# The eight gate columns from the unnormalised input, in four column groups of TensorE

## The chip, the cores and the metric

The kernel runs on one core of a Trainium2 chip. The metric is the device time of one execution in microseconds (us). TensorE is called PE here, VectorE DVE, ScalarE ACT, GpSimd POOL and SyncE SP.

## The reference, cut to what matters

One inference step of a hybrid decoder layer over 592 rows: 16 meta tokens, 512 prompt tokens and 8 samples of 8 tokens. All data are fp32.

```
xn = x * rsqrt(mean(x*x) + eps) * g              # g = norm1_g
z  = xn @ w_in + b_in                            # 1024 inner
u, q, k, v, o, ipre, fpre, ga, gb = split(z)     # ipre, fpre: 4 columns each, one per head
uc = causal_conv4(u); ha = RG-LRU(uc)            # gates of 16 diagonal blocks, then a scan
hb = mLSTM(q, k, v, ipre, log_sigmoid(fpre))
merged = sigmoid(ga)*(ha @ w_branch_a) + sigmoid(gb)*(hb @ w_branch_b)
x = x + merged @ w_out;  x = x + ConvFFN(RMSNorm(x));  y = RMSNorm(x)
```

The change is about the eight columns `ipre` and `fpre`, called the gates below. The mLSTM needs them much later than the first 50 us.

## The kernel before, in words

The input lies transposed in SBUF, features on the 128 partitions, 592 rows along the free dimension, as 8 tiles of 128 features. A large product is made from three fast (fp32r) products: the weight is split in a high part (`whi`) and a low part (`wlo`), the input in `xh` and `xl`, and high*high, high*low and low*high are summed in PSUM. One unit tile of 128 output columns is one `gemm`: 8 k-steps of 3 products, each in two column halves, 48 matmuls (line 2063). Its weight comes by DMA into `stage`, ACT copies it into `whi` (`hi`, line 963) once the tile two before is done, POOL subtracts to get `wlo` (`lo`, line 905, counted by `w_lo`). ACT evicts the tile. Two PSUM areas of two banks (`wide[0]`, `wide[1]`) alternate by the tile's number; four more banks (`bank`) serve everything else.

The start of the kernel, up to the second unit tile, is written out by hand, in order, for each engine:

- PE turns the raw input (`turn`, `late_turn`, line 2101). It is done in 16 jobs: job n is feature tile n % 8, columns 0 to 255 for n < 8 (part 0) and 256 to 591 for n >= 8 (part 1).
- For each job ACT keeps the raw data (`raw_copy`, line 1015, into `x_raw`), DVE scales them out of PSUM by norm1_g and by the row `rrow` of inverse roots (`xn_scaled`, line 1432, `tile_evicted`), ACT rounds to `xh` (`xn_high`, line 1027), and POOL (part 0, line 917) or DVE (part 1, line 1468, `xn_lo_b`) makes `xl`. PSUM has four slots for these jobs, so `late_turn(n)` waits for the scaling of job n - 4.
- Between the turns PE does the gates (`gate_step`, 16 steps of three matmuls with 36 stationary columns; ten of them stand ahead of `late_turn(15)`) and the first unit tile (`first_step`, 16 steps of three), both in line 2110. A gate step or first step of job n waits for that job's `xl`.
- `row_transposes` (line 2091) turns 15 tiles of parameter rows into PSUM in two groups; ACT copies them into `cols` (`columns`, line 1033).
- `keep_clock` are transposes whose result nobody reads.

Then the unit tiles 1 to 15 follow in a loop over g. Ahead of g = 3 stands `lru_gates(0)` (line 2209), which uses all four banks of `bank` and waits for `conv(0)`.

On DVE, after the last `xl`, the order is: copies from `cols`, `lru_rates()`, `conv(0)`, `conv(1)`, and then the loop. `lru_rates` sends |lambda| to ACT, waits for ACT's exp (`lam_exp`, line 1090), and goes on with some twenty operations on 8 columns, each waiting for the one before. `conv(f)` is one TENSOR_SCALAR (line 1552) and three SCALAR_TENSOR_TENSOR (line 1432) over 616 columns and waits for the eviction of unit tile f.

On ACT, after the 16 jobs: `hi(2)` (line 963), `columns` of both groups, the two evictions of the gates into `gs` (lines 1085, 1087), the exp of lambda, and then for each g: `lru_period(g)`, `main_hi(g)` (the split of weight g + 3, which waits for the end of unit tile g), and the eviction of unit tile g.

Of the kernel before, what the change touches and what calls it, by code (L numbers as in the profile page):

```python
# [31 lines left out]
P = 128  # L32
KT = D // P
# [54 lines left out]
T_GATE = T_COLS2 + 2  # L88
T_U = T_GATE + 1
# [167 lines left out]
def hybrid_layer(nc, a, o):  # L257
    w_in, b_in = a["w_in"][0], a["b_in"][0]
    ctx = ExitStack()
    with ctx:  # L260
# [128 lines left out]
        ghi, glo = whi3[:, 0:KT * GATE_W], wlo3[:, 0:KT * GATE_W]  # L389

        def gate_columns(ap):

            return bass.AP(ap.tensor, ap.offset, [ap.ap[0], [GATE_W, KT], [32, 2], [1, HEADS]])
# [118 lines left out]
        rms_done, x_sq = sem("rms_done"), sem("x_sq")  # L512
        lam_abs, lam_exp, gate_abs, gate_exp, gates_ready = (
# [357 lines left out]
        def _(pool):  # L871
# [9 lines left out]
            st(pool.memset(ghi.bitcast(F32), 0.0))  # L881
            st(pool.memset(glo.bitcast(F32), 0.0))
# [19 lines left out]
            def lo(b, slot, n):  # L902

                pool.wait_ge(w_hi, b + 1)
                pool.tensor_tensor(spaced(wlo[:, slot]), packed(stage[:, slot, 0:n]), spaced(whi[:, slot]).bitcast(F32),  # L905
                                   ALU.subtract).then_inc(w_lo, 1)
# [6 lines left out]
            def xn_low(n):  # L913
# [8 lines left out]
            pool.wait_ge(w_hi, 1)  # L922
            pool.tensor_tensor(gate_columns(glo), gate_in_w.rearrange("p k (g h) -> p k g h", h=HEADS),
                               gate_columns(ghi).bitcast(F32), ALU.subtract).then_inc(w_lo, 1)
            for n in range(2, 8):
                xn_low(n)
            pool.wait_ge(w_lo, 2)
# [15 lines left out]
            for i in range(2 * B_HALF):  # L943
                b = B_FFN + i
                w_, l_ = ffn_weight(i)
                pool.wait_ge(w_hi, b + 1)
# [8 lines left out]
        def _(act):  # L955
# [93 lines left out]
            for n in range(2):  # L1049
                xn_high(n)  # L1050
                raw_copy(n + 4)
            act.wait_ge(gate_w_in, 16)
            act.wait_ge(const_done, 2)
            act.activation(gate_columns(ghi), gate_in_w.rearrange("p k (g h) -> p k g h", h=HEADS), ACT.Copy
                           ).then_inc(w_hi, 1)
# [25 lines left out]

            t = T_GATE
            act.wait_ge(gate_rows_in, 48)
            act.wait_ge(tile_done, t + 1)
# [342 lines left out]
        def _(dve):  # L1427
# [58 lines left out]
            dve.wait_ge(w_hi, 2)  # L1486
# [120 lines left out]
            def gates_abs():  # L1607

                dve.wait_ge(tile_evicted, T_GATE + 1)
# [71 lines left out]
            conv(0)  # L1681
            conv(1)
# [207 lines left out]
            dve.wait_ge(w_hi, b + 1)  # L1890
# [157 lines left out]
        def _(pe):  # L2048
# [65 lines left out]
            def gate_step(part, kk):  # L2114

                pe.wait_ge(w_lo, 1)
                return part_step(bank2(0), GATE_W, GATE_W, ghi, glo, kk, part)

            def first_step(part, kk):

                pe.wait_ge(w_lo, 2)
                pe.wait_ge(rb_ready, 2)
                return part_step(bank2(1), P, WS, whi[:, 1], wlo[:, 1], kk, part)
# [36 lines left out]
            gate_step(0, 0)  # L2160
            rms_rows(1)
            late_turn(8)
            late_turn(9)
            gate_step(0, 1)
            late_turn(10)
            late_turn(11)
            gate_step(0, 2)
            gate_step(0, 3)
            gate_step(0, 4)
            late_turn(12)  # L2170
            gate_step(0, 5)
            late_turn(13)
            gate_step(0, 6)
            gate_step(0, 7)
            gate_step(1, 0)
            late_turn(14)
            first_step(0, 0)
            first_step(0, 1)
            gate_step(1, 1)
            late_turn(15)  # L2180
            for kk in range(2, 8, 2):
                first_step(0, kk)
                first_step(0, kk + 1)
                if kk < 6:
                    gate_step(1, 1 + kk // 2)
# [38 lines left out]
            for g in range(1, 16):  # L2224
                if g in LRU_TURN:
                    lru_gates(LRU_TURN.index(g))
                gemm(B_U + g, T_U + g, (B_U + g) % 2, (T_U + g) % 2, KT, xh, xl, m0=0 if g < 8 else M0,
                     free=T_COLS2 + 1 if g == 1 else None)
# [351 lines left out]
```

## Time and profile before

| | |
|---|---|
| time, median of 3 | 1067.67 us (1067.43 to 1068.07) |
| time of the profiled execution | 1067.82 us |
| its span, first to last instruction | 1066.0 us |
| PE busy | 1054.0 us (99%) |
| DVE busy | 620.0 us (58%) |
| ACT busy | 388.5 us (36%) |
| POOL busy | 371.1 us (35%) |
| granted TensorE clock, mean | 0.999 of full speed |

The profiled execution's time is 1.82 us above its span: what lies around the first and the last instruction. Times below are counted from the start of the span. A timeline row gives start, length, engine, line, operation, output and inputs with their sizes, the number of instructions merged into the row, and in brackets the idle time ahead of it with what ended it. A PE row's length holds the last matmul's passage through the array, so the pace is read from start to start. A row of the windows gives the stretch, its length, the busy time of PE, PE's weight loads, DVE, ACT and POOL with their instructions, the granted clock (1.00 is full), the DMA share and GB/s.

### The profile page before, as it was taken

The numbers are of one execution on the slowest core, as the hardware profiler recorded it, in microseconds if no ns is written. First come the engines' busy times: TensorE is split into PE (matmuls) and PEld (weight loads), VectorE is DVE, ScalarE is ACT, GpSimd is POOL, SyncE is SP. The second block draws the span as 40 slices with busy tenths as digits, with TensorE's granted clock in tenths as the row PEclk, the third lists the DMA queues.
The fourth block names the chain that finished last, engine by engine and source line by source line (L and its number), as shares of the span: only waits on it lengthen the run. The fifth ranks groups of instructions, "written<-read, shape, count | busy, mean of one in ns | idle before, by whom it ended". The sixth has DMA issues, their size and how long they took to land.

```text
span 1066.0 us, 19415 instructions
## 1 busy us (share of the span) xinstructions
PE 1054.0 (99%) x7974; PEld 1029.3 (97%) x7974; DVE 620.0 (58%) x971; ACT 388.5 (36%) x562; POOL 371.1 (35%) x180
## 2 busy tenths in 40 slices
PE   7999999999999999999999999999999999999997
PEld 6999999999999999999999999999999999999997
DVE  6777457854533343442543339999940189999413
ACT  6566787313332333232422333222211122222332
POOL 4333344333222222222223344334443344334330
PEclk9999999999999999999999999999999999999999
DMA  7433322346385592863443232322323222233312
GB/s 198 164 102 92 103 75 78 85 104 163 85 231 154 129 263 62 195 197 90 149 163 88 81 99 86 93 80 80 102 71 103 62 80 80 81 93 99 98 44 89
DMA packets 215696, 119.67 MB, mean 112 GB/s; under 512 B 39195, under 2 KB 212235, under 8 KB 215358
## 3 DMA queue, kind: packets, MB, share of 16 engines
q1 hardware_dynamic: 215404, 118.42, 39.4%
q8 instruction: 63, 1.03, 0.4%
q14 instruction: 19, 0.16, 0.0%
q10 hardware_dynamic: 210, 0.07, 0.0%
HBM read 97.49 MB, written 18.76 MB: 109 GB/s over the span
## 4 chain that ended last, share of the span: by engine, by line
PE 98%; ACT 1%; DMA 0%; POOL 0%; DVE 0%; issue 0%; SPq 0%; DVEq 0%
PE ring L2063 48%; PE ring L2481 22%; PE bank L2481 17%; PE bank L2353 2%; PE bank L2340 1%; PE bank L2110 1%; PE bank L2321 1%; PE bank L2333 1%; PE bank L2395 1%; PE bank L2220 1%; PE bank L2383 1%; PE bank L2418 0%; DMA x_tok<-in_x_prompt 0%; POOL x_split L917 0%; ACT sq_tok L1000 0%; PE bank L2527 0%
## 5 line engine op out<-in xcount | busy, mean ns | idle before, releaser
L2063 PE MATMUL ring<-x_split,whi 128*128 128x256 f32 (+1 forms) x2016 | 359.2, 300 | 0.0
L905 POOL TENSOR_TENSOR wlo<-stage,whi 128x1024 fp32r<-128x1024 f32 x78 | 194.2, 2490 | 411.7 <-ACT whi L963 411.7
L2063 PEld LDWEIGHTS ring<-x_split,whi 128*128 128x128 f32 x2016 | 303.9, 189 | 8.1 <-issue 7.6
L2063 PE MATMUL ring<-x_split,wlo 128*128 128x256 f32 (+1 forms) x1008 | 217.4, 297 | 0.0
L2063 PEld LDWEIGHTS ring<-x_split,wlo 128*128 128x128 f32 x1008 | 169.9, 189 | 0.0
L963 ACT ACTIVATE whi<-stage 128x1024 fp32r<-128x1024 f32 x80 | 84.3, 1054 | 92.3 <-PE ring L2063 81.2
L948 POOL TENSOR_TENSOR wlo<-stage,whi 128x1024 fp32r<-128x1024 f32 x28 | 71.7, 2560 | 108.4 <-ACT whi L1316 108.4
L2481 PE MATMUL ring<-x_split,whi 128*128 128x256 f32 (+1 forms) x512 | 88.7, 295 | 0.0
L1432 DVE SCALAR_TENSOR_TENSOR conv<-up,cols,conv 128x592 f32<-128x592 f32 x88 | 75.5, 858 | 3.1
L2481 PEld LDWEIGHTS ring<-x_split,whi 128*128 128x128 f32 x512 | 77.0, 189 | 0.0
L1969 DVE TENSOR_SCALAR conv<-up,cols 128x592 f32<-128x592 f32 x44 | 74.0, 1683 | 3.1
L2481 PE MATMUL bank<-x_split,whi 128*128 128x256 f32 (+1 forms) x384 | 66.5, 295 | 0.0
L948 POOL TENSOR_TENSOR wlo_third<-stage,whi_third 128x1024 fp32r<-128x1024 f32 x16 | 40.8, 2550 | 58.4 <-ACT whi_third L1316 58.4
L1819 DVE COPY num_tok<-bank 128x257 f32<-128x257 f32 x20 | 8.5, 426 | 86.1 <-PE bank L2340 67.7
L2481 PEld LDWEIGHTS bank<-x_split,whi 128*128 128x128 f32 x384 | 57.8, 189 | 0.0
L1352 ACT ACTIVATE conv<-conv 128x592 f32<-128x592 f32 x22 | 15.4, 702 | 115.8 <-DVE conv L1432 115.8
L951 POOL TENSOR_TENSOR wlo<-stage,whi 128x1408 fp32r<-128x1408 f32 x12 | 38.7, 3228 | 52.3 <-ACT whi L1318 52.3
L2481 PE MATMUL ring<-x_split,wlo 128*128 128x256 f32 (+1 forms) x256 | 54.8, 296 | 0.0
L1316 ACT ACTIVATE whi<-stage 128x1024 fp32r<-128x1024 f32 x28 | 29.5, 1055 | 65.0 <-PE ring L2481 43.0
L2013 DVE TENSOR_TENSOR resid<-ring,resid 128x576 f32<-128x576 f32 x9 | 6.8, 758 | 68.9 <-PE ring L2481 68.9
L2481 PE MATMUL ring<-x_split,whi_third 128*128 128x256 f32 (+1 forms) x256 | 44.6, 296 | 0.0
L2481 PE MATMUL bank<-x_split,whi_third 128*128 128x256 f32 (+1 forms) x256 | 44.4, 295 | 0.0
(365 smaller groups left out, 2053.3 us busy)
## 6 DMA issues: line engine op xcount, KB each, us to landing
stage<-in_w_in SPq DMA_DIRECT2D x56, 512.0 KB, 4.0
stage<-in_w_up SPq DMA_DIRECT2D x44, 512.0 KB, 3.7
stage<-in_w_down SPq DMA_DIRECT2D x16, 704.0 KB, 4.5
stage<-in_w_branch_a SPq DMA_DIRECT2D x8, 512.0 KB, 3.7
c_sample<-in_state_mlstm_C SPq DMA_DIRECT2D x16, 256.0 KB, 6.2
out_s_mlstm_C<-c_sample SPq DMA_DIRECT2D x16, 256.0 KB, 2.4
stage<-in_w_branch_b SPq DMA_DIRECT2D x8, 512.0 KB, 3.9
stage<-in_w_out SPq DMA_DIRECT2D x8, 512.0 KB, 3.8
```

The lines of the kernel that those rows point to most:

```text
L905: pool.tensor_tensor(spaced(wlo[:, slot]), packed(stage[:, slot, 0:n]), spaced(whi[:, slot]).bitcast(F32), ALU.subtract).then_inc(w_lo, 1)
L948: pool.tensor_tensor(spaced(l_), packed(stage[:, b % 2, 0:D]), spaced(w_).bitcast(F32), ALU.subtract).then_inc(w_lo, 1)
L951: pool.tensor_tensor(l_, stage[:, b % 2, :], w_.bitcast(F32), ALU.subtract).then_inc(w_lo, 1)
L963: act.activation(spaced(whi[:, slot]), packed(stage[:, slot, 0:n]), ACT.Copy).then_inc(w_hi, 1)
L1316: act.activation(spaced(ffn_weight(i)[0]), packed(stage[:, b % 2, 0:D]), ACT.Copy).then_inc(w_hi, 1)
L1352: act.activation(cv[:, 1, 0:CV_N], cv[:, 1, 0:CV_N], ACT.Gelu_apprx_tanh).then_inc(gelu_done, 1)
L1432: return stt(out=out, in0=in0, scalar=scalar, in1=in1, op0=op0, op1=op1)
L1969: st.link(ts(c_, U[:, 0:CV_N], w[0], bias, ALU.mult, ALU.add))
L2063: last = pe.matmul(of(z, t0 or -2, t1), w[:, kk * WS:kk * WS + P], x_, start=kk == 0 and m == 0, stop=kk == kn - 1 and m == 2)
L2110: last = pe.matmul(of_first(z, t0, t1)[0:M], w[:, step * kk:step * kk + M], x[:, f, t0:t1], start=kk == 0 and m == 0, stop=kk == KT - 1 an ...
L2353: lz = pe.matmul(ZP[:, ii], kw[kappa % 3][:, P * ii:P * ii + P], vt[s][:, c, :], start=True, stop=True, skip_group_check=True)
L2481: last = pe.matmul(out(z, t0, t1), w_[:, kk * step:kk * step + P], x_[:, kk, t0 - at:t1 - at], start=kk == 0 and m == 0, stop=kk == kn - 1 ...
```

## The change

**Gate products.** The eight gate columns no longer use the split, normalised input. `gate_w` is the gates' weight times norm1_g, in plain fp32, padded to 32 columns (POOL makes it in place of the low part). `gate_products`, behind the first unit tile, multiplies the raw input `x_raw` by it: 8 feature tiles by two halves of 296 columns, 16 plain fp32 matmuls, feature tile kk in column group kk % 4 of the array, so that four partial sums lie on the partitions 0-31, 32-63, 64-95 and 96-127 of two banks.

**Scaling and sum.** DVE multiplies these partial sums by `rrow` into `gate_z` (behind `conv(0)`), and PE sums the four groups with a 0/1 matrix `gate_sel` (`gate_sums`, two plain fp32 matmuls of 296 columns, ahead of unit tile 2). `gate_sel` is made on POOL by three additions of pieces of the identity.

**Moves.** ACT loses the gates' high copy and evicts the gates in its turn for g = 2, ahead of `main_hi(2)`. The first unit tile goes to `bank2(0)`. The late turns come closer together on PE, and the parameter rows' transposes stand ahead of the first unit tile's last step instead of ahead of four gate steps. Tile numbers fall by one behind the parameter rows, so unit tile 1 takes the other PSUM area and waits for both groups of `columns`. `w_hi` counts one less.

```diff
 # POOL
-            st(pool.memset(ghi.bitcast(F32), 0.0))
-            st(pool.memset(glo.bitcast(F32), 0.0))
+            st(pool.memset(gate_w[:, :, :], 0.0))
+            st(pool.memset(gate_sel[:, :], 0.0))
...
-            pool.wait_ge(w_hi, 1)
-            pool.tensor_tensor(gate_columns(glo), gate_in_w.rearrange("p k (g h) -> p k g h", h=HEADS),
-                               gate_columns(ghi).bitcast(F32), ALU.subtract).then_inc(w_lo, 1)
+            pool.wait_ge(gate_w_in, 16)
+            pool.wait_ge(tile_evicted, T_COLS + 1)
+            pool.tensor_tensor(gate_w[:, :, 0:2 * HEADS], gate_in_w, cols[:, C_N1:C_N1 + KT]...to_broadcast([P, KT, 2 * HEADS]), ALU.mult).then_inc(w_lo, 1)
             for n in range(2, 8):
                 xn_low(n)
+            st.link(pool.tensor_tensor(sel, gate_rows_of(ident[:, :], 0), gate_rows_of(ident[:, :], 1), ALU.add))
+            st.link(pool.tensor_tensor(sel, sel, gate_rows_of(ident[:, :], 2), ALU.add))
+            pool.tensor_tensor(sel, sel, gate_rows_of(ident[:, :], 3), ALU.add).then_inc(gate_sel_ready, 1)
 # ACT
-            act.activation(gate_columns(ghi), gate_in_w..., ACT.Copy).then_inc(w_hi, 1)
...
-            st(act.activation(gs[:, 0, :], of_first(bank2(0))[0:HEADS], ACT.Identity, bias=gbias[:, 0:1]))
-            act.wait_ge(tile_evicted, t)
-            act.activation(gs[:, 1, :], of_first(bank2(0))[32:32 + HEADS], ACT.Copy).then_inc(tile_evicted, 1)
             act.wait_ge(lam_abs, 1)
             act.activation(lam[0], lam[0], ACT.Exp, scale=-1.0).then_inc(lam_exp, 1)
...
+            def gate_evict():
+                act.wait_ge(gate_rows_in, 48)
+                act.wait_ge(gate_summed, 1)
+                st(act.activation(by_halves(gs[:, 0, :]), bank[0:HEADS, 2:4, 0:T // 2], ACT.Identity, bias=gbias[:, 0:1]))
+                act.activation(by_halves(gs[:, 1, :]), bank[32:32 + HEADS, 2:4, 0:T // 2], ACT.Copy
+                               ).then_inc(gate_evicted, 1)
             for g in range(31):
                 if g:
                     lru_period(g)
+                if g == 2:
+                    gate_evict()
                 main_hi(g)
 # DVE
             lru_rates()
             conv(0)
+            dve.wait_ge(gate_psum, 1)
+            dve.wait_ge(rb_ready, 2)
+            tt(by_halves(gate_z[:, :]), bank[:, 2:4, 0:T // 2], by_halves(rrow[:, :]), ALU.mult).then_inc(gate_scaled, 1)
             conv(1)
 # PE
+            def gate_products():
+                pe.wait_ge(w_lo, 1)
+                pe.wait_ge(raw_done, XN)
+                pe.wait_ge(rb_ready, 2)
+                for hf in range(2):
+                    for kk in range(KT):
+                        j = kk % 4
+                        last = pe.matmul(bank[32 * j:32 * j + 32, 2 + hf, 0:T // 2], gate_w[:, kk, :],
+                                         x_raw[:, kk, T // 2 * hf:T // 2 * hf + T // 2], start=kk < 4, stop=kk >= 4,
+                                         tile_position=(0, 32 * j), skip_group_check=True)
+                last.then_inc(gate_psum, 1)
+            def gate_sums():
+                pe.wait_ge(gate_sel_ready, 1)
+                pe.wait_ge(gate_scaled, 1)
+                for hf in range(2):
+                    last = pe.matmul(bank[0:GATE_W, 2 + hf, 0:T // 2], gate_sel[:, :],
+                                     gate_z[:, T // 2 * hf:T // 2 * hf + T // 2], start=True, stop=True)
+                last.then_inc(gate_summed, 1)
...
-            gate_step(0, 0)
             rms_rows(1)
-            late_turn(8)
...
+            for n in range(8, 12):
+                late_turn(n)
             first_step(0, 0)
             first_step(0, 1)
+            late_turn(12)
+            first_step(0, 2)
+            first_step(0, 3)
+            late_turn(13)
+            first_step(0, 4)
+            first_step(0, 5)
+            late_turn(14)
+            first_step(0, 6)
+            first_step(0, 7)
             late_turn(15)
+            for kk in range(7):
+                first_step(1, kk)
             for n in range(2):
                 row_transposes(T_COLS2 + n, *COL_GROUPS[n])
-            for kk in (4, 5, 6):
-                gate_step(1, kk)
-            gate_step(1, 7).then_inc(tile_done, 1)
-            for kk in range(7):
-                first_step(1, kk)
             first_step(1, 7).then_inc(tile_done, 1)
+            gate_products()
...
             def lru_gates(p):
                 pe.wait_ge(conv_done, p + 1)
                 if p:
                     pe.wait_ge(lru_sig, p)
                 else:
                     pe.wait_ge(bd_in, 96)
                     pe.wait_ge(tile_evicted, T_U + 1)
+                    pe.wait_ge(gate_evicted, 1)
...
             for g in range(1, 16):
                 if g in LRU_TURN:
                     lru_gates(LRU_TURN.index(g))
+                elif g == 2:
+                    gate_sums()
-                gemm(B_U + g, ..., free=T_COLS2 + 1 if g == 1 else None)
+                gemm(B_U + g, ..., free=T_COLS2 + 2 if g == 1 else None)
```

## Rows read from the trace of the kernel before

**Rows 1.** the page, busy time of each engine
```profile
...
PE 1054.0 (99%) x7974; PEld 1029.3 (97%) x7974; DVE 620.0 (58%) x971; ACT 388.5 (36%) x562; POOL 371.1 (35%) x180
...
```

**Rows 2.** windows: one stretch with the busy us of each engine
```profile
...
120.00:1066.00 946.00, 940.17 (x7127) 923.06 (x7125) 536.68 (x828) 310.46 (x425) 324.82 (x129) 1.00 0.39 109
...
```

**Rows 3.** chain of waits, first 60 us: start us, us, engine, tile, line
```profile
...
23.79 3.13 PE bank L2110 x24
26.92 1.47 PE ring L2091 x15
28.39 5.61 PE bank L2110 x36
34.00 13.20 PE ring L2063 x96
47.20 2.07 PE bank L2209 x8
...
```

**Rows 4.** timeline of DVE, 26 to 32 us: start us, us, operation
```profile
...
26.48 1.15 DVE L1468 TENSOR_TENSOR x_split<-xn_full,x_split 128x336 fp32r<-128x336 f32 x2
...
29.21 1.40 DVE L1524 TENSOR_SCALAR misc<-cols 128x8 f32<-128x8 f32 x1 [1.55 <-ACT cols L1033]
...
31.18 0.16 DVE L1432 SCALAR_TENSOR_TENSOR misc<-cols 128x8 f32<-128x8 f32 x1
...
```

**Rows 5.** timeline of PE, 3 to 41 us
```profile
...
3.07 2.40 PE L2084 MATMUL bank<-ident 128*128 128x128 f32 x10
...
12.31 1.25 PE L2084 MATMUL bank<-ident 128*128 128x128 f32 x10
...
23.34 0.45 PE L2101 MATMUL ring<-ident,x_tok 128*128 128x128 f32 x3
...
33.84 0.72 PE L2063 MATMUL ring<-x_split,whi 128*128 128x272 f32 x4
...
40.47 0.70 PE L2063 MATMUL ring<-x_split,whi 128*128 128x272 f32 x4
...
```

**Rows 6.** timeline of ACT, 27 to 50 us
```profile
...
27.95 2.32 ACT L1033 ACTIVATE cols<-ring 128x128 f32<-128x128 f32 x15
...
31.77 1.28 ACT L1090 ACT_TABLE_LOAD   x1
33.06 0.21 ACT L1090 ACTIVATE misc<-misc 128x8 f32<-128x8 f32 x1
...
40.73 1.06 ACT L963 ACTIVATE whi<-stage 128x1024 fp32r<-128x1024 f32 x1 [4.63 <-PE ring L2063]
...
49.35 1.28 ACT L1104 ACT_TABLE_LOAD   x1 [0.20 <-PE bank L2209]
...
```

**Rows 7.** chain of waits, 295 to 306 us
```profile
...
300.97 1.86 PE bank L2383 x32
...
```

**Rows 8.** timeline of DVE, 35 to 67 us
```profile
...
35.37 2.30 DVE L1432 SCALAR_TENSOR_TENSOR misc<-misc 128x8 f32<-128x8 f32 x1
...
39.19 0.59 DVE L1552 TENSOR_SCALAR uc<-u,cols 128x616 f32<-128x616 f32 x1
39.82 2.65 DVE L1432 SCALAR_TENSOR_TENSOR uc<-u,cols,uc 128x616 f32<-128x616 f32 x3
...
62.28 4.68 DVE L1432 SCALAR_TENSOR_TENSOR uc<-u,cols,uc 128x616 f32<-128x616 f32 x3
...
```

**Rows 9.** timeline of POOL, 35 to 67 us
```profile
...
35.24 2.41 POOL L905 TENSOR_TENSOR wlo<-stage,whi 128x1024 fp32r<-128x1024 f32 x1 [4.65 <-ACT whi L963]
...
63.69 2.61 POOL L905 TENSOR_TENSOR wlo<-stage,whi 128x1024 fp32r<-128x1024 f32 x1 [4.16 <-ACT whi L963]
...
```

**Rows 10.** instructions of line 2013: ns min/median/max, first and last start
```profile
...
L2013 DVE TENSOR_TENSOR resid<-ring,resid x9: 757/758/758, 801.1 to 1045.7; 128x576 f32<-128x576 f32 x9
...
```

**Rows 11.** windows at the end of the span
```profile
...
1060.00:1061.00 1.00, 0.17 (x2) 0.00 (x0) 0.88 (x2) 0.76 (x2) 0.00 (x0) 1.00 1.01 410
...
1064.00:1065.00 1.00, 0.00 (x0) 0.00 (x0) 0.00 (x0) 0.00 (x0) 0.00 (x0) 0.61 0.63 234
...
```

More of the change, by code:

```diff
@@ L87 @@
 T_COLS2 = T_XN + XN
-T_GATE = T_COLS2 + 2
-T_U = T_GATE + 1
+T_U = T_COLS2 + 2
 T_GA = T_U + 8
@@ L388, in hybrid_layer, with by_halves, gate_rows_of @@
         gate_in_w = stage[:, 0, D + 296:D + 296 + 8 * KT].rearrange("p (k c) -> p k c", c=8)
-        ghi, glo = whi3[:, 0:KT * GATE_W], wlo3[:, 0:KT * GATE_W]
-        def gate_columns(ap):
-            return bass.AP(ap.tensor, ap.offset, [ap.ap[0], [GATE_W, KT], [32, 2], [1, HEADS]])
+        gate_w = sb("gate_w", [P, KT, 32], o_p - 2 * SLOT - 64)
+        gate_sel = sb("gate_sel", [P, GATE_W], o_p - SLOT - 64)
+        gate_z = sb("gate_z", [P, T], o_b + 7 * TB)
+        def by_halves(ap):
+            return ap.rearrange("p (h t) -> p h t", h=2)
+        def gate_rows_of(ap, j):
+            return bass.AP(ap.tensor, ap.offset + 32 * j, [ap.ap[0], [HEADS, 2], [1, HEADS]])
         def spaced(w):
@@ L512, in hybrid_layer @@
         rms_done, x_sq = sem("rms_done"), sem("x_sq")
+        gate_sel_ready, gate_psum, gate_scaled, gate_summed, gate_evicted = (
+            sem("gate_sel_ready"), sem("gate_psum"), sem("gate_scaled"), sem("gate_summed"), sem("gate_evicted"))
         lam_abs, lam_exp, gate_abs, gate_exp, gates_ready = (
@@ L921, in _ @@
             xn_low(1)
[L922 to L924 removed]
+            pool.wait_ge(gate_w_in, 16)
+            pool.wait_ge(tile_evicted, T_COLS + 1)
+            pool.tensor_tensor(gate_w[:, :, 0:2 * HEADS], gate_in_w,
+                               cols[:, C_N1:C_N1 + KT].rearrange("p (k o) -> p k o", o=1).to_broadcast([P, KT, 2 * HEADS]),
+                               ALU.mult).then_inc(w_lo, 1)
             for n in range(2, 8):
                 xn_low(n)
+            sel_ = gate_sel[:, :]
+            sel = bass.AP(sel_.tensor, sel_.offset, [sel_.ap[0], [32, 2], [1, HEADS]])
+            st.link(pool.tensor_tensor(sel, gate_rows_of(ident[:, :], 0), gate_rows_of(ident[:, :], 1), ALU.add))
+            st.link(pool.tensor_tensor(sel, sel, gate_rows_of(ident[:, :], 2), ALU.add))
+            pool.tensor_tensor(sel, sel, gate_rows_of(ident[:, :], 3), ALU.add).then_inc(gate_sel_ready, 1)
             pool.wait_ge(w_lo, 2)
@@ L945, in _ @@
                 w_, l_ = ffn_weight(i)
-                pool.wait_ge(w_hi, b + 1)
+                pool.wait_ge(w_hi, b)
                 if i % B_HALF < 2 * HK:
@@ L1051, in _ @@
                 raw_copy(n + 4)
[L1052 to L1055, printed above, removed]
             square_tile(4)
@@ L1485, in _ @@
                 xn_scaled(n)
-            dve.wait_ge(w_hi, 2)
+            dve.wait_ge(w_hi, 1)
             dve.wait_ge(w_lo, 1)
@@ L1607, in gates_abs @@
             def gates_abs():
-                dve.wait_ge(tile_evicted, T_GATE + 1)
+                dve.wait_ge(gate_evicted, 1)
                 st.link(ts(f_, f_, gbias[:, 1:2], None, ALU.add))
@@ L1889, in _ @@
             b = B_WB + 1
-            dve.wait_ge(w_hi, b + 1)
+            dve.wait_ge(w_hi, b)
             dve.wait_ge(w_lo, b)
@@ L2112, in part_step @@
                 return last
-            def gate_step(part, kk):
+            def gate_products():
                 pe.wait_ge(w_lo, 1)
-                return part_step(bank2(0), GATE_W, GATE_W, ghi, glo, kk, part)
+                pe.wait_ge(raw_done, XN)
[14 more added lines that the diff above has]
+                last.then_inc(gate_summed, 1)
             def first_step(part, kk):
                 pe.wait_ge(w_lo, 2)
-                pe.wait_ge(rb_ready, 2)
-                return part_step(bank2(1), P, WS, whi[:, 1], wlo[:, 1], kk, part)
+                return part_step(bank2(0), P, WS, whi[:, 1], wlo[:, 1], kk, part)
             for n in range(4):
@@ L2159, in _ @@
             keep_clock(10)
-            gate_step(0, 0)
             rms_rows(1)
-            late_turn(8)
[L2163 to L2176, printed above, removed]
+            for n in range(8, 12):
+                late_turn(n)
             first_step(0, 0)
             first_step(0, 1)
-            gate_step(1, 1)
-            late_turn(15)
[L2181 to L2185, printed above, removed]
+            late_turn(12)
[7 more added lines that the diff above has]
+            first_step(0, 7)
+            late_turn(15)
+            for kk in range(7):
+                first_step(1, kk)
             pe.wait_ge(rows_in[0], 16 * 7)
@@ L2226, in _ @@
                     lru_gates(LRU_TURN.index(g))
+                elif g == 2:
+                    gate_sums()
                 gemm(B_U + g, T_U + g, (B_U + g) % 2, (T_U + g) % 2, KT, xh, xl, m0=0 if g < 8 else M0,
-                     free=T_COLS2 + 1 if g == 1 else None)
+                     free=T_COLS2 + 2 if g == 1 else None)
             def fill(h, n, ks=range(KT)):
```

7 lines of the change are left out of this document (2 added, 5 removed).

## The prediction

> **What bounds the kernel now.** I read four views, in this order. The page's busy times first: PE has work for 1054.0 of 1066.0 us [rows 1]. Then the windows: from 120 us to the end PE is busy for 940.17 of 946.00 us, and the rest is the tail behind its last instruction [rows 2, 11]. So from the second unit tile on PE is a queue without gaps, and whatever moves the start of that queue moves the end by as much. Third the chain of waits over the first 60 us: from 23.79 us on it has only PE pieces, among them the 36 matmuls of line 2110 in 5.61 us (12 of the gates, 24 of the first unit tile) and, between unit tiles 2 and 3, the eight of line 2209 [rows 3]. Fourth the timelines. Two marks count: unit tile 1 starts at 33.84 us and unit tile 2 at 40.47 us, so one unit tile takes 6.63 us [rows 5]. I take the start of unit tile 2 as the mark for the whole time, because behind it PE's work is the same in both kernels and nothing waits.
>
> **What is removed on PE.** 48 gate matmuls. Those of 256 columns follow each other at 3.13/24 = 0.13 us, those of 336 at 5.61/36 = 0.156 us [rows 3]: 24 of each make 3.1 + 3.7 = 6.9 us. Part of the first half filled waits for `xl`, so less than that is gained.
>
> **What is added on PE.** The 16 plain fp32 matmuls of `gate_products` are two instructions each, 32 in all. The nearest row is the state product of the mLSTM: the same number, plain fp32, 32 stationary columns in four column groups, 256 moving columns, 1.86 us [rows 7]. With 296 columns: 1.86 x 296/256 = 2.15 us. If the groups did not overlap, each instruction would cost what one of line 2209 does, 2.07/8 x 296/308 = 0.25 us, and 32 of them 8.0 us [rows 3]; I take 2.15, since the row is of the same form. `gate_sums` is four such instructions over the full array: 1.0 us.
>
> **Up to unit tile 1.** Ahead of `late_turn(15)` (23.34 us [rows 5]) stood ten gate steps and two first steps, now eight first steps: four steps fewer at 3 x 0.13 us, 1.5 us. DVE's scaling lets 1.2 us of this through. ACT's gate copy is gone too (0.14 us there). The last `xl`, finished at 27.6 us before [rows 4], comes at 26.3 us. PE's second last first step ends at about 26.1 us, the transposes take 1.47 us [rows 3], the last step 0.46 us, the gate products 2.15 us: PE is free for unit tile 1 at 30.15 us. `columns` starts when its first eight transposes are done, at 27.05 instead of 27.95 us, takes 2.32 us [rows 6] and so has both groups out at 29.4 us; the weight's low part is ready about then as well. So unit tile 1 starts at 30.15 us, 3.7 us earlier, and ends at 36.8 us. If the story ended here, the kernel would be 2.7 us faster (3.7 less the 1.0 of `gate_sums`).
>
> **The wait that is added.** PE's next instruction is `gate_sums`, which waits for `gate_scaled`. On DVE that stands behind all of `lru_rates` and `conv(0)`. Behind PE's wait stand unit tile 2 and everything after it. When is DVE there?
>
> - Lambda to ACT: DVE's operation at 31.18 us came behind one that had been held to 30.6 us, the end of POOL's subtraction for weight 2 [rows 4]. That subtraction follows ACT's `hi(2)`, which comes 1.2 us earlier with the last `xh`. So this operation is at 30.0 us.
> - ACT is idle by then (the evictions of the gates are gone) and loads the table of exp, 1.28 us, and does the exp, 0.21 us. The row at 49.35 us shows that a table load stands behind the wait, not ahead of it [rows 6]. `lam_exp` is at 31.5 us, 1.8 us before its old 33.27.
> - From `lam_exp` to `conv(0)` it was 39.19 - 33.27 = 5.92 us [rows 6, 8]. In this lies one operation on 8 columns that took 2.30 us instead of its usual 0.17, alongside POOL's subtraction of 35.24 to 37.65 us [rows 8, 9]. POOL's next subtraction again comes a good 1 us behind `lam_exp`, since ACT's `hi(3)` follows the exp. So 5.92 us stays: 37.4 us.
> - `conv(0)` takes 39.82 + 2.65 - 39.19 = 3.28 us without disturbance [rows 8]: 40.7 us. But `hi(4)` starts 0.26 us behind the end of unit tile 1 and takes 1.06 us [rows 5, 6], so POOL's subtraction for weight 4 starts at about 38.2 us, in the middle of `conv(0)`. The row at 62.28 us is the same conv with a POOL subtraction at 63.69 us: 4.68 instead of 2.65 us [rows 8, 9]. This adds 2.03 us: 42.7 us.
> - The scaling reads 592 columns from PSUM. The nearest row, 576 columns from PSUM, is 0.758 us [rows 10], so 0.78 us: `gate_scaled` at 43.5 us.
>
> PE idles from 36.8 to 43.5 us. With `gate_sums` unit tile 2 starts at 44.55 instead of 40.47 us: +4.1 us.
>
> **The clock.** PE's last instruction ends at 1060.17 us, and the granted clock goes from 1.00 to the mean of 0.61 in the window from 1064 us: it falls to half at about 1064.2 us, 4.0 us after PE stopped [rows 11]. At the start, ten transposes take 2.40 us and later 1.25 us [rows 5]: half speed, for 2.4 us at least, until PE had worked a while. An idle time of 6.7 us is beyond 4.0 us, so I expect the clock to be at 1.2 GHz when `gate_sums` starts: it takes 2.0 instead of 1.0 us, and then about 1 us of unit tile 2 at half speed costs 0.5 us more. +1.5 us; bounds 0 (it doesn't fall) and 3 us (an estimate: 6 us at half speed). The Trainium skill's page "TensorE: Matmul & The Clock Gate" speaks against this change in its section "Why this matters for your kernels": it warns of idle gaps between bursts of matmuls, since the clock drops back. By that rule the change costs 5.6 us, without it 4.1 us; the end of this trace agrees with it.
>
> **Costed at nothing.** ACT's two evictions of the gates (1.4 us) move behind `gate_sums`, under unit tile 2 with its 6.6 us; without that cover `lru_gates(0)` would wait for them. `conv(1)`, which `lru_gates(1)` needs at g = 6, comes 1 to 2 us later beside a PE that is later by more. POOL's new multiplication replaces a subtraction of the same 64 columns; its three additions lie in POOL's gap ahead of weight 2. SP issues the same transfers in the same order.
>
> **The sum.** The profiled execution took 1067.82 us for a span of 1066.0 us. 1067.82 + 4.1 + 1.5 = 1073.4 us. The median of the runs is 0.15 us below it, so 1073.3 us.
>
> **The rivals.**
>
> 1. *As forecast, but the clock stays up.* For it: nothing in this trace shows a fall in mid-kernel. Against it: the 4.0 us at the end. +4.1 us, 1071.8 us. 18%.
> 2. *POOL's subtraction spares `conv(0)`*, because DVE's operations follow each other closely and POOL waits instead. The row of POOL's operation at 63.69 us speaks against it. `gate_scaled` at 41.5 us, +2.1 us, and with a clock that falls in 4.7 us of idle time +3.6: 1069.8 to 1071.3 us. 13%.
> 3. *The other side: the scaling isn't late.* One mechanism: the eight-column operations of `lru_rates` and `conv(0)` run without either hold (2.13 and 2.03 us) and start earlier than I think. From `gate_scaled` at 39.4 us on down there is no loss, and at 36.8 us the full gain is there: 2.7 us less, 1064.9 us. It needs DVE to be there 6.7 us before my sum, of which the two holds are 4.2. 4% for faster, and 4% that it ends within 0.2% with hold and stall about even.
> 4. *Later still.* The rows' transposes now come 0.6 us earlier and may have to wait for the last parameter rows' transfer; then `columns`, lambda and the scaling shift by as much; or the clock needs long to rise. +7 to +9 us, 1075 to 1077 us. 9%.
>
> My forecast has the remaining 52%.
>
> **How the numbers follow.** Faster by over 0.2% (2.1 us, about what a measurement of this kernel can tell from no change): 3%. Within 0.2%: 7%, from rivals 3 and the low end of 2. Slower: 90%. The range takes in rival 2 from its middle up, rival 1, the forecast and its clock's bounds (1071.8 to 1074.8), and the lower end of rival 4: 1069.6 to 1075.4 us.
>
> **What would show it.** In the profile after: unit tile 1's first matmul near 30.2 us; the gate products as 32 instructions in about 2.2 us; one idle time of PE of 6 to 7 us ahead of `gate_sums`, released by DVE's scaling; the granted clock below 1.00 in the windows behind it; a conv(0) of 5.3 us with POOL's subtraction inside it; no new idle time later. Wrong would be: unit tile 2 starting before 40.5 us, the gate products near 8 us, or a stall of PE elsewhere.

## The result, and the profile after

The changed kernel takes 1075.32 us (median of 4, 1074.14 to 1077.5) against 1067.87 us for the kernel before: ratio 1.0069, 95% interval 1.0057 to 1.0081. It is slower by 7.45 us; 5.6 us had been forecast. The profiled execution is the fastest of the four, 1074.14 us with a span of 1072.3 us, 6.3 us above the profiled execution of before.

The page after has the same busy time of PE over a longer span, so PE is idle for 18.3 us in all instead of 12.0 us. What the missing gate matmuls save in busy time is taken up by the added ones and by matmuls at the slow clock:

```profile
...
span 1072.3 us, 19382 instructions
...
PE 1054.0 (98%) x7962; PEld 1026.1 (96%) x7962; DVE 619.0 (58%) x972; ACT 388.0 (36%) x561; POOL 372.1 (35%) x183
...
```

The timeline of PE from the last first steps to the first `lru_gates` (line numbers moved: 2107 are the rows' transposes, 2138 the gate products, 2079 a unit tile, 2148 `gate_sums`, 2229 the first `lru_gates`):

```profile
...
26.11 0.54 PE L2126 MATMUL bank<-x_split,whi 128*128 128x336 f32 x2 [0.20 <-DVE x_split L1481]
...
26.69 1.67 PE L2107 MATMUL ring<-ident,rows 128*128 128x128 f32 x15
...
28.78 2.20 PE L2138 MATMUL bank<-x_raw,gate_w 128*32 128x296 f32 x32
30.91 0.81 PE L2079 MATMUL ring<-x_split,whi 128*128 128x272 f32 x4
...
37.37 0.44 PE L2079 MATMUL ring<-x_split,wlo 128*128 128x272 f32 x2
44.14 2.16 PE L2148 MATMUL bank<-gate_z,gate_sel 128*36 128x296 f32 x4 [6.33 <-DVE gate_z L1697]
46.23 1.24 PE L2079 MATMUL ring<-x_split,whi 128*128 128x272 f32 x4
...
53.37 1.20 PE L2229 MATMUL bank<-uc,lru_w_r 128*128 128x308 f32 x4
...
```

The same mark in the timeline of the kernel before, where `lru_gates` is line 2209:

```profile
...
47.04 1.20 PE L2209 MATMUL bank<-uc,lru_w_r 128*128 128x308 f32 x4
...
```

Unit tile 1 starts at 30.91 us against 33.84 us [rows 5], so the gain of the shorter start is there. It ends at 37.8 us, and then the row of `gate_sums` has 6.33 us of idle time ahead of it, released by DVE's scaling. The timeline of DVE shows what came first:

```profile
...
25.47 1.14 DVE L1481 TENSOR_TENSOR x_split<-xn_full,x_split 128x336 fp32r<-128x336 f32 x2
...
29.51 0.17 DVE L1537 TENSOR_SCALAR misc<-cols 128x8 f32<-128x8 f32 x1 [2.86 <-ACT cols L1047]
...
30.25 0.16 DVE L1445 SCALAR_TENSOR_TENSOR misc<-cols 128x8 f32<-128x8 f32 x1
...
33.18 3.77 DVE L1445 SCALAR_TENSOR_TENSOR misc<-misc 128x8 f32<-128x8 f32 x8
...
38.07 0.59 DVE L1565 TENSOR_SCALAR uc<-u,cols 128x616 f32<-128x616 f32 x1
38.69 4.61 DVE L1445 SCALAR_TENSOR_TENSOR uc<-u,cols,uc 128x616 f32<-128x616 f32 x3
43.22 0.77 DVE L1697 TENSOR_TENSOR gate_z<-bank,rms_row 128x592 f32<-128x592 f32 x1
...
```

The scaling (line 1697) stands behind `conv(0)` (lines 1565, 1445). The eight operations of 8 columns take 3.77 us and the three of `conv(0)` 4.61 us instead of 2.65 [rows 8]. The timeline of POOL has its subtraction in both places:

```profile
...
33.12 2.41 POOL L912 TENSOR_TENSOR wlo<-stage,whi 128x1024 fp32r<-128x1024 f32 x1 [3.57 <-ACT whi L977]
39.03 2.72 POOL L912 TENSOR_TENSOR wlo<-stage,whi 128x1024 fp32r<-128x1024 f32 x1 [3.51 <-ACT whi L977]
...
```

The timeline of ACT, with `columns` (1047), exp of lambda (1093), the split of weight 4 (977), and the gates' copies (1231, 1232), which now wait for `gate_sums`:

```profile
...
28.25 2.32 ACT L1047 ACTIVATE cols<-ring 128x128 f32<-128x128 f32 x15 [1.23 <-PE ring L2107]
30.59 1.28 ACT L1093 ACT_TABLE_LOAD   x1
31.88 0.21 ACT L1093 ACTIVATE misc<-misc 128x8 f32<-128x8 f32 x1
...
37.90 1.06 ACT L977 ACTIVATE whi<-stage 128x1024 fp32r<-128x1024 f32 x1 [4.07 <-PE ring L2079]
...
46.39 0.75 ACT L1231 ACTIVATE gate_scratch<-bank,misc 4x592 f32<-4x592 f32 x1 [6.63 <-PE bank L2148]
47.16 0.66 ACT L1232 ACTIVATE gate_scratch<-bank 4x592 f32<-4x592 f32 x1
...
```

Last the windows around the idle time (columns as in [rows 2]):

```profile
...
38.00:40.00 2.00, 0.00 (x0) 0.00 (x0) 1.93 (x4) 1.76 (x3) 0.96 (x1) 1.00 0.35 104
40.00:41.00 1.00, 0.00 (x0) 0.00 (x0) 1.00 (x1) 0.00 (x0) 1.00 (x1) 0.68 0.03 8
41.00:42.00 1.00, 0.00 (x0) 0.00 (x0) 1.00 (x1) 0.00 (x0) 0.75 (x1) 0.50 0.00 0
...
46.00:47.00 1.00, 1.00 (x4) 0.78 (x4) 0.96 (x2) 0.61 (x1) 0.00 (x0) 0.50 0.00 0
47.00:48.00 1.00, 1.00 (x9) 1.00 (x8) 0.40 (x3) 0.80 (x2) 0.00 (x0) 0.91 0.00 0
...
```

The granted clock is full at 38 to 40 us and 0.68 in the window from 40 us, so it fell to half (0.50, 1.2 GHz) at about 40.4 us, 2.6 us after PE stopped. It rose at about 47.2 us (0.91 in the window from 47 us), 3.0 us after PE had started again. `gate_sums` and the start of unit tile 2 ran at half speed.

### The profile page after: what moved, and what is told of

It reads as the page before. It is cut to its first block, busy times and chain, and to the rows that moved or that the text cites. A ratio compares the mean times of both kernels' runs of the same rounds, so it can differ in the third digit from the quotient of the medians.

```text
span 1072.3 us, 19382 instructions
## 1 busy us (share of the span) xinstructions
PE 1054.0 (98%) x7962; PEld 1026.1 (96%) x7962; DVE 619.0 (58%) x972; ACT 388.0 (36%) x561; POOL 372.1 (35%) x183
## 4 chain that ended last, share of the span: by engine, by line
PE 96%; DVE 1%; ACT 1%; DMA 0%; issue 0%; SPq 0%; DVEq 0%; ACTq 0%
PE ring L2079 47%; PE ring L2503 22%; PE bank L2503 17%; PE bank L2375 2%; PE bank L2362 1%; PE bank L2343 1%; PE bank L2355 1%; PE bank L2417 1%; PE bank L2240 1%; PE bank L2405 1%; PE bank L2440 0%; DMA x_tok<-in_x_prompt 0%; PE bank L2126 0%; DVE uc L1445 0%; DVE misc L1445 0%
## 5 line engine op out<-in xcount | busy, mean ns | idle before, releaser
L1985 DVE TENSOR_SCALAR conv<-up,cols 128x592 f32<-128x592 f32 x44 | 70.0, 1591 | 3.1
L965 POOL TENSOR_TENSOR wlo<-stage,whi 128x1408 fp32r<-128x1408 f32 x12 | 38.6, 3226 | 52.6 <-ACT whi L1331 52.6
L1973 DVE COPY up<-cols 128x16 f32<-128x16 f32 x44 | 44.8, 1018 | 0.0
```

The costliest lines, as they stand in the source:

```text
L1973: st(cpy(grouped(U[:, US0:UW_F - UG], UG)[:, :, 0:FW - 1], hist[:, :, ft:ft + UPT + 1:UPT]))
L1985: st.link(ts(c_, U[:, 0:CV_N], w[0], bias, ALU.mult, ALU.add))
```

## Experiments

The yardstick is the stretch from the start of `gate_sums` to the start of line 2229 (the first `lru_gates`; the line number moves a little with the edits). With the clock at full speed it is 7.85 us (in e2 and e4, below). In the changed kernel it is 53.37 - 44.14 = 9.23 us, so the clock cost 1.4 us in this execution. From the start of `lru_gates` to the end, all profiled executions, the one before too, take 1018.8 to 1019.1 us: whatever differs lies ahead of that mark. Times are medians; the kernel before, on the same chips, had 1068.2 us for e1 to e4, 1068.28 us for a1, e5, e6 and e7, and 1067.95 us for e8 and e9.

### a1: the changed kernel again

> The changed kernel itself, in more rounds and on one chip with the three below, as their base. 1075.3 us; runs spread over about 3 us, against less than 1 us for the kernel before, since the granted clock falls in the idle time and the stretch at half speed is not equally long in each run.

1075.29 us (5 runs, 1074.08 to 1076.45), ratio 1.0067 [1.0053, 1.008]. Its profiled execution has 6.31 us of idle time at the same place and a stretch of 9.30 us. So the result came again. Two rows of its PE timeline:

```profile
...
32.07 0.82 PE L2079 MATMUL ring<-x_split,whi 128*128 128x272 f32 x4
...
45.28 2.16 PE L2148 MATMUL bank<-gate_z,gate_sel 128*36 128x296 f32 x4 [6.31 <-DVE gate_z L1697]
...
```

Unit tile 1 starts at 32.07 us here and at 30.91 us in the first profile, and this 1.16 us is the whole difference between the two executions (1075.29 and 1074.14 us). It is there by 12 us, where PE had waited 0.98 us instead of 0.18 us for the first transfer of the input and had run some early transposes at a slower pace. In the other runs unit tile 1 starts anywhere from 30.37 us (e1) to 31.81 us (e8), with the same work ahead of it (e5 apart, whose products are longer). So two profiled executions are compared by stretches, not by their times.

### e1: the scaling ahead of `conv(0)`

```diff
             lru_rates()
-            conv(0)
             dve.wait_ge(gate_psum, 1)
             dve.wait_ge(rb_ready, 2)
             tt(by_halves(gate_z[:, :]), ..., ALU.mult).then_inc(gate_scaled, 1)
+            conv(0)
             conv(1)
```

> The changed kernel with one move on DVE: the scaling of the gates stands ahead of conv(0) instead of behind it. My theory (the wait of gate_sums for DVE sets the start of unit tile 2, and the clock's fall comes on top): the scaling runs at about 38.1 us, gate_sums starts at 38.9 us, unit tile 2 at 39.9 us after an idle time of PE of some 1.2 us; the granted clock stays at full speed; 1067.4 us, 0.5 below the kernel before and 8 below the changed one. Rival (the gate products and sums are themselves what costs, the wait only covers it): at most 2 us below the changed kernel, 1073 us or more.

1067.47 us (10 runs), ratio 0.9995 [0.9986, 1.0004]: as expected to 0.1 us. PE's timeline:

```profile
...
38.15 1.16 PE L2148 MATMUL bank<-gate_z,gate_sel 128*36 128x296 f32 x4 [0.88 <-DVE gate_z L1696]
...
45.97 1.20 PE L2229 MATMUL bank<-uc,lru_w_r 128*128 128x308 f32 x4
...
```

One operation of 0.77 us, moved by one place in DVE's queue, is worth 7.8 us in the medians. Of this the profiles show 5.45 us less idle time of PE (0.88 instead of 6.33 us) and 1.4 us of the clock, which stays up (a stretch of 7.82 us); 0.5 us more is an earlier start of unit tile 1. The gate products and sums ran as in the changed kernel, so they are not what makes it slower.

### e2: the clock kept up

```diff
                 pe.wait_ge(gate_sel_ready, 1)
+                pe.wait_ge(tile_evicted, T_U + 1)
+                keep_clock(44)
                 pe.wait_ge(gate_scaled, 1)
```

> The changed kernel with 44 transposes on PE, whose result nobody reads, in the idle time ahead of gate_sums; the wait itself stays as long. Theory (the fall of the granted clock is a cost of its own, 1.6 us in the profile, more in the slower runs): no window below 1.00, gate_sums in 1.0 instead of 2.1 us, unit tile 2 at about 45.1 us instead of 46.2 us and 6.6 instead of 7.1 us long; 1072.5 us, with the runs within 1 us of each other. Rival (the clock costs nothing that counts): 1075.3 us as the changed kernel, with the same spread of 3 us.

1073.31 us (4 runs, 1072.62 to 1073.45), ratio 1.0045 [1.003, 1.0061]. The windows show 1.00 from 2 to 60 us, and PE's timeline:

```profile
...
38.41 4.97 PE L2100 MATMUL bank<-ident 128*128 128x128 f32 x44
44.83 1.19 PE L2150 MATMUL bank<-gate_z,gate_sel 128*36 128x296 f32 x4 [1.46 <-DVE gate_z L1697]
...
52.68 1.20 PE L2231 MATMUL bank<-uc,lru_w_r 128*128 128x308 f32 x4
...
```

`gate_sums` and unit tile 2 take 52.68 - 44.83 = 7.85 us. The wait itself ends as late as it did: 13.16 us behind the start of unit tile 1 (at 31.67 us), 13.21 us in a1. 2.0 us of the median are gone, and most of the spread. The profiled executions of a1 and e2 differ by 1.9 us in their spans; 1.45 us of it is the stretch, and 0.45 us is how much earlier `gate_sums` starts (44.83 against 45.28 us). So the clock is a cost of its own, 1.4 us where the profiles show it.

### e3: POOL's subtraction behind `conv(0)`

```diff
-            los(3, B_WA + 5, D)
+            lo(3, 1, D)
+            pool.wait_ge(conv_done, 1)
+            lo(4, 0, D)
+            los(5, B_WA + 3, D)
```

> The changed kernel with one wait more on POOL: its subtraction for weight 4 waits for the end of conv(0), so that the two do not meet. Theory (POOL's subtraction holds conv(0) up by 2 us and PE waits for conv(0)): the three operations of conv(0) take 2.65 instead of 4.6 us, gate_sums starts at about 42.2 us; 1073.3 us if the clock still falls, 1071.7 us if the shorter idle time of 4.3 us spares it. Rival (the hold is not on PE's path, since POOL and DVE share nothing that counts): 1075.3 us.

1073.14 us (4 runs, 1072.56 to 1074.45), ratio 1.005 [1.0035, 1.0065]. DVE's timeline has the three operations at their usual length:

```profile
...
38.32 2.65 DVE L1448 SCALAR_TENSOR_TENSOR uc<-u,cols,uc 128x616 f32<-128x616 f32 x3
...
```

The hold is gone, 1.96 us. PE's timeline and the windows:

```profile
...
41.80 2.16 PE L2151 MATMUL bank<-gate_z,gate_sel 128*36 128x296 f32 x4 [4.36 <-DVE gate_z L1700]
...
51.84 1.20 PE L2232 MATMUL bank<-uc,lru_w_r 128*128 128x308 f32 x4
...
```

```profile
...
39.00:40.00 1.00, 0.00 (x0) 0.00 (x0) 0.96 (x2) 0.39 (x2) 0.00 (x0) 0.98 0.00 0
40.00:41.00 1.00, 0.00 (x0) 0.00 (x0) 0.96 (x3) 0.00 (x0) 0.00 (x0) 0.50 0.00 0
...
46.00:47.00 1.00, 1.00 (x6) 1.00 (x6) 0.54 (x3) 0.00 (x0) 0.00 (x0) 0.61 0.52 155
...
```

PE starts again at 41.80 us, but the clock fell all the same, at about 40.0 us, and rose at 46.8 us. The stretch takes 10.04 us: the clock costs 2.2 us here, 0.8 us more than in the two profiles of the changed kernel (9.23 and 9.30 us), because PE came back sooner into a low stretch of the same length. In these executions a shorter wait gave back part of what it won. The medians don't show it: from a1 to e3 they fall by 2.1 us, which is the whole hold.

### e7: e2 and e3 together

The edit of e3, and that of e2 with `keep_clock(28)`.

> e2 and e3 together: POOL's subtraction for weight 4 behind conv(0), and 28 unread transposes on PE in the idle time. Theory (hold and clock are two costs that add; in e3 the hold was gone, 2.0 us, but the clock's low stretch then lay over more of PE's work, 5 us instead of 3, and took back 1 us): no window below 1.00, gate_sums in 1.0 us at about 41.9 us, unit tile 2 at 42.9 us; 1070.9 us, 2.3 below e3. Rival (e3 gained 2 us by the hold alone and the clock is worth 1.6 us in both): 1071.5 us or more.

1070.88 us (6 runs, 1070.3 to 1073.08), ratio 1.0026 [1.0015, 1.0038]: the expected time. The clock was at 1.00 in the wait and behind it, and the stretch takes 7.79 us. With the clock kept up, the hold on `conv(0)` is worth 2.4 us (e2 to e7), and in e3 the clock was worth 2.3 us (e3 to e7). By the medians with a falling clock the hold was worth 2.1 us; these differences of a few tenths are too small for four to six runs to tell apart. What stays is the wait for a `conv(0)` that nothing disturbs: 2.6 us above the kernel before. One thing in its profile was not expected: the granted clock was at 0.50 from 16.5 to 19.9 us, long before the wait, and the work from 15.7 us to the start of unit tile 1 took 0.9 us longer than in e3.

### e9: a longer wait

```diff
             lru_rates()
             conv(0)
+            conv(1)
             dve.wait_ge(gate_psum, 1)
             ...
-            conv(1)
```

> The changed kernel with the scaling behind conv(1) as well: 3.3 us more of DVE's work ahead of it, so that PE idles for some 9.7 us instead of 6.4. Theory (unit tile 2 follows DVE's scaling one to one, and the clock rises only once PE has worked for some 3 us, so the clock's cost stays): gate_sums in 2.1 us at about 48.6 us, 1078.6 us. Rival (the low stretch has a length of its own, 6.8 us in both profiles so far, and would be over when PE starts again): gate_sums in 1.0 us, 1077.0 us.

1078.47 us (4 runs), ratio 1.0099 [1.0083, 1.0114]: 3.2 us above a1 for 3.3 us more of DVE's work. In the profiles the start of `gate_sums` lies 16.51 us behind that of unit tile 1 (30.59 us), against 13.23 us: also 3.3 us more. PE's timeline and windows:

```profile
...
47.10 2.16 PE L2148 MATMUL bank<-gate_z,gate_sel 128*36 128x296 f32 x4 [9.61 <-DVE gate_z L1698]
...
57.41 1.20 PE L2229 MATMUL bank<-uc,lru_w_r 128*128 128x308 f32 x4
...
```

```profile
...
42.00:43.00 1.00, 0.00 (x0) 0.00 (x0) 0.96 (x4) 0.00 (x0) 0.00 (x0) 0.66 0.31 41
...
52.00:53.00 1.00, 1.00 (x8) 1.00 (x7) 0.00 (x0) 0.00 (x0) 0.00 (x0) 0.72 0.00 0
...
```

The low stretch is longer here, from about 42.3 to 52.6 us, so 6.8 us is not its fixed length, and the clock was still low when PE started again. The rival fell. The theory's "some 3 us" of work before the rise doesn't hold either: PE had worked again for 5.5 us. The stretch from `gate_sums` takes 10.31 us, 2.5 us of it for the clock.

### e4: the scaling in DVE's idle time

```diff
                 mul_add(lam[0], L_, -1.0, L_, ALU.mult, ALU.max).then_inc(lam_abs, 1)
+                dve.wait_ge(gate_psum, 1)
+                dve.wait_ge(rb_ready, 2)
+                tt(by_halves(gate_z[:, :]), ..., ALU.mult).then_inc(gate_scaled, 1)
                 dve.wait_ge(lam_exp, 1)
```

(and gone from behind `conv(0)`)

> The changed kernel with the scaling of the gates in DVE's idle time between its request for exp of lambda and the answer. Theory: the products are done at 30.9 us and DVE is idle till about 32.1 us, so the scaling costs DVE nothing, gate_sums follows unit tile 1 without a wait, unit tile 2 starts at 38.7 us against 40.5 us in the kernel before; 1066.0 us, 1.8 below the kernel before. Rival (something else at the same place waits as well: gate_sel, the area of unit tile 2, the gates' copy ahead of lru_gates(0)): between 1067 and 1070 us, with an idle time of PE of 1 us or more before unit tile 3.

1066.55 us (11 runs, 1066.32 to 1069.99), ratio 0.9989 [0.998, 0.9998]: faster than both kernels, by 1.65 us against the one before on its chip. The time is 0.5 us above the expected one, the gain nearly the expected 1.8 us. DVE's timeline, then PE's:

```profile
...
30.80 0.16 DVE L1445 SCALAR_TENSOR_TENSOR misc<-cols 128x8 f32<-128x8 f32 x1
31.62 0.78 DVE L1551 TENSOR_TENSOR gate_z<-bank,rms_row 128x592 f32<-128x592 f32 x1 [0.66 <-PE bank L2138]
...
```

```profile
...
31.48 0.82 PE L2079 MATMUL ring<-x_split,whi 128*128 128x272 f32 x4
...
38.31 1.19 PE L2148 MATMUL bank<-gate_z,gate_sel 128*36 128x296 f32 x4
39.43 0.82 PE L2079 MATMUL ring<-x_split,whi 128*128 128x272 f32 x4
...
46.16 1.20 PE L2229 MATMUL bank<-uc,lru_w_r 128*128 128x308 f32 x4
...
```

PE has no idle time between the gate products and line 2229. Two of the eleven runs are above 1068 us (1068.8 and 1069.99 us); their mean granted clock is 0.996, that of the other nine 0.998 or 0.999, so the clock was low for longer in them, though no profile shows where. One place is seen in the profiled execution, in its windows:

```profile
...
16.00:17.00 1.00, 1.00 (x7) 0.90 (x7) 1.00 (x4) 1.00 (x3) 0.25 (x1) 0.59 0.94 134
...
19.00:20.00 1.00, 1.00 (x8) 1.00 (x7) 0.36 (x1) 1.00 (x3) 1.00 (x2) 0.70 0.21 58
...
```

The clock was at half speed from about 16.2 to 19.6 us, in the late turns; the profiles of e1 and of the kernel before show 1.00 there. From the start of these turns to that of unit tile 1 it took 15.32 us, in e1 14.83 us, so this cost about 0.5 us. Together with a wait of PE for DVE at 14.2 us, 0.4 us longer than in e1, this is most of the 1.1 us by which unit tile 1 starts later than there.

### e5: one column group

e4 with all gate products in the first 32 columns of the array, accumulated over the eight feature tiles:

```diff
-                        j = kk % 4
-                        last = pe.matmul(bank[32 * j:32 * j + 32, 2 + hf, 0:T // 2], gate_w[:, kk, :], ...,
-                                         start=kk < 4, stop=kk >= 4, tile_position=(0, 32 * j), skip_group_check=True)
+                        last = pe.matmul(bank[0:32, 2 + hf, 0:T // 2], gate_w[:, kk, :], ..., start=kk == 0, stop=kk == KT - 1)
```

> The kernel of e4 (scaling in DVE's idle time) with all 16 gate products in one column group, accumulated over the eight feature tiles; scaling and sum take the 32 partitions that are left. Theory (four column groups work at the same time, as the state product's rows showed): the 32 instructions take 32 x 0.247 = 7.9 us instead of 2.15 us, and all of it is on PE's path: e4 + 5.7 us, 1072.3 us. Rival (the array isn't the limit of these products but the instructions' issue or the reading of x_raw): e4 + at most 2 us, 1068.5 us.

1072.32 us (5 runs, 1071.92 to 1072.43), ratio 1.0035 [1.0022, 1.0049], 5.8 us above e4. PE's timeline:

```profile
...
28.81 8.16 PE L2137 MATMUL bank<-x_raw,gate_w 128*32 128x296 f32 x32
36.90 0.81 PE L2079 MATMUL ring<-x_split,whi 128*128 128x272 f32 x4
...
```

From start to start 8.09 us against 2.13 us in four groups. The page "TensorE: Matmul & The Clock Gate" of the Trainium skill says in "Part 3: Packing small matmuls — row/col tiling" that small products in distinct column groups run at the same time; the runs agree, with a factor of 3.8.

### e6: the gates' copy behind `main_hi(2)`

```diff
-                if g == 2:
-                    gate_evict()
                 main_hi(g)
+                if g == 2:
+                    gate_evict()
```

> The kernel of e4 with the gates' copy out of PSUM behind main_hi(2) on ACT instead of ahead of it. main_hi(2) waits for the end of unit tile 2, so the copy's cover is gone. Theory: lru_gates(0) waits for 1.06 us of main_hi(2) and 1.4 us of the two copies, PE idles some 2.6 us ahead of line 2209, the clock stays: 1069.1 us, e4 + 2.6. Rival (lru_gates(0) has slack elsewhere, the order on ACT is indifferent): 1066.6 us as e4.

1070.57 us (9 runs, 1068.92 to 1073.27), ratio 1.0021 [1.0011, 1.003]. PE's timeline of the profiled execution:

```profile
...
48.00 1.27 PE L2229 MATMUL bank<-uc,lru_w_r 128*128 128x308 f32 x4 [2.61 <-ACT gate_scratch L1232]
...
```

The 2.61 us of idle time came as expected, and this execution (1068.92 us) has the expected time, with the clock at 1.00. The median is 1.5 us above. The mean granted clock of the runs says more: the five slowest of the nine (1070.57 to 1073.27 us) have 0.994 to 0.997, the four others 0.998 or 0.999. So the clock was low for longer in most of the slower runs, but not in one of 1070.35 us.

### e8: e6 with the clock kept up

e6 with `keep_clock(18)` ahead of the wait for `gate_evicted`.

> The kernel of e6 with 18 unread transposes on PE ahead of lru_gates(0)'s wait for the gates' copy. In e6 PE idled for 2.6 us there, the profiled execution kept its clock and was the fastest of nine (1068.9 us), and the median was 1070.6 us. Theory (2.6 us is about where the clock falls, and it fell in most of e6's executions but not in the profiled one): with the transposes all executions are like the profiled one, 1069.1 us, spread below 1 us. Rival (e6's other runs were slow for another reason): 1070.6 us and a spread of some 4 us as e6.

1069.33 us (11 runs, 1068.65 to 1071.62), ratio 1.0013 [1.0004, 1.0023]. Against the kernel before on its chip it is 1.4 us slower, e6 was 2.3 us slower. The median is near the expected 1069.1 us, the spread stayed wider than expected (ten runs within 1.3 us, one at 1071.62 us). Ten of the eleven runs have a mean granted clock of 0.998 or more, and the one far off has 0.996, against five of nine below 0.998 in e6. That the clock fell in about half of e6's runs agrees with this; that it fell in PE's idle time ahead of `lru_gates(0)` is likely but not shown, since no profile caught it.

## Why the prediction was right, and where its sizes were off

**The mechanism is shown.** PE's wait in `gate_sums` for DVE's scaling, which stands behind `lru_rates` and `conv(0)`, decides the time: e1 moves the scaling by one place and takes away 7.8 us, e9 moves it the other way and adds 3.2 us, one to one with DVE's work. The chance of 90% for slower went to the right side. That the range of 1069.6 to 1075.4 us holds 1075.32 us, by 0.08 us, is partly luck: the forecast's own bounds ended at 1074.8 us, and the rest was there for rival 4. Part of that rival came true, `columns`, lambda and the scaling shifted together, but not for its reason: PE didn't wait for a transfer of the rows.

**What was added on PE.** The gate products take 2.13 us from start to start, forecast 2.15, from the row of the same form [rows 7]. `gate_sums` costs 1.28 us (7.85 less the 47.04 - 40.47 = 6.57 us of unit tile 2 before), forecast 1.0: in e4 1.12 us pass from its start to that of unit tile 2, and unit tile 2 itself takes 0.16 us longer. Unit tile 1 behind the gate products is 0.2 us longer as well (6.83 us in e4, 6.63 us before). Neither was in the sum.

**Up to unit tile 1.** Forecast 30.15 us, measured 30.91. The last `xl` ended at 26.6 us (forecast 26.3), the second last first step started at 26.11 us, so the transposes started at 26.69 instead of 26.1 us. The later transposes are 0.6 of the 0.76 us by which unit tile 1 is late. `columns` started at 28.25 instead of 27.05 us: half of this is the later transposes, half that it came 1.56 us behind the first of them, where I had allowed 0.95 us. ACT waited for them (1.23 us in its row). This start of `columns` is the term that was mis-sized.

**The wait.** ACT could load the table only at 30.59 us, when `columns` was out; I had it wait for DVE's request at 30.0 us (it came at 30.25). So `lam_exp` came at 32.09 us (forecast 31.5), `conv(0)` at 38.07 us (37.4), with one held operation in between as forecast; `conv(0)` ended at 43.3 us (42.7), held up by 1.96 us (2.03); the scaling took 0.77 us (0.78) and `gate_sums` started at 44.14 us (43.5). Every step after `lam_exp` has its forecast length; all start 0.6 us late. With `gate_sums` at 1.28 us, unit tile 2 would end 44.14 + 7.85 - 47.04 = 4.95 us later than before at full clock; 4.1 us had been forecast.

**The two holds.** e3 shows the one on `conv(0)`: with POOL out of the way its operations take 2.65 us again. The one on the eight-column operations (2.1 us) was in every profile, beside POOL's subtraction, and wasn't removed, so its cause is read and not tested. The Trainium skill's page "SBUF — State Buffer" says in "Who interferes with whom" that DVE and POOL share a pair of ports under an exclusive lock; the trace agrees, as an operation of 0.17 us that meets POOL's subtraction lasts 2.37 us. Rival 2, in which POOL waits instead, fell: POOL's subtraction beside `conv(0)` took 2.72 us, 0.3 us more than alone.

**The clock.** Forecast 1.5 us with bounds 0 and 3. The two profiled executions of the changed kernel lost 1.4 us, e3 2.2 us and e9 2.5 us by their stretches. The step was right, and so was its size. 4.95 + 1.4 = 6.3 us is the whole difference of the two spans. The prediction also read half speed at the start of the kernel before out of ten transposes in 2.40 us; the windows over 3 to 6 us show 1.00 there, so the slower pace is on record but not its cause.

**Why the median is higher still.** The median is 7.45 us above, not 6.3 us. a1's profiled execution has this time, and its span is 7.5 us above: 1.16 us because unit tile 1 starts later than in the first profile, 4.95 us, and 1.45 us for the clock. The forecast knew the start of the kernel from one execution only and had no term for how much it varies. Whether the kernel before has the same variation isn't shown by a profile; its runs on these chips, one far-off run left out, spread over 1.4 to 1.7 us.

**Where the gain went.** It is real, but it was paid into a wait. Without the wait (e4) the change brings 1.65 us in the medians. The first profile would give 2.93 us from the earlier unit tile 1, less 1.28 us for `gate_sums` and 0.2 us for the longer unit tile 1, some 1.45 us. e4's profiled execution, with its low clock at 16 us, won only 0.9 us up to the mark (46.16 against 47.04 us). The forecast had 2.7 us for this case.

**Costed at nothing.** That the gates' copies lie under unit tile 2 held; e6 takes the cover away and PE idles for 2.61 us. POOL's additions and SP's queue cost nothing that the profile shows.

## What to carry to other kernels

When work is split into product, scaling and sum over three engines, find out where each engine's queue stands at that moment: a scaling of 0.77 us behind 11 us of other operations stops TensorE for 6 us, and the same scaling in an idle time one wait earlier costs nothing (e4). When the wait of a busy TensorE is shortened but not removed, look at the granted clock behind it: in e3's profile it cost 0.8 us more than with the longer wait. Take a second profile of the same kernel before you read a difference of 1 us between two: here the start alone moved by 1.16 us. Small products belong in separate column groups (e5).

## What the runs showed of the hardware that I had not expected

- The granted clock fell 2.6 us (changed kernel), 2.5 us (e3), 2.8 us (a1) and 4.8 us (e9) after PE's last matmul, against 4.0 us at the end of the kernel before. In e6 PE idled for 2.61 us, and the clock stayed at 1.00.
- It can also fall without such an idle time. In e4 and e7 it fell at 16.2 and 16.5 us, while PE was busy; the longest idle time of PE in the 4 us before was 1.05 us in e4 and 0.62 us in e7, and e1 and e3, with the same 0.62 us, kept their clock. Both low stretches lasted 3.4 us.
- The low stretches were 6.8 us (changed kernel, a1, e3) and 10.2 us (e9), and PE worked for 3.0, 3.3, 5.0 and 5.5 us of them. What the clock costs goes with this overlap, not with the idle time: e3, with the shortest idle time (4.36 us), lost more than the changed kernel with 6.33 us.
- The spread of the runs is in part a sign of the clock: 3.4 us in the changed kernel, whose slowest run has a mean granted clock of 0.992 and the others 0.995 or 0.996, and 0.8 us in e2, with 0.998 to 1.000. The other part is the start of the kernel, which moved by 1.16 us between two profiles whose windows show 1.00 there.
